# Interleaving attention steps with projection tiles in a two-block transformer kernel on Trainium2: four parts per step instead of two, single-tile slices, and a new home for the head transposes

## What is computed

```python
p = rms_norm(x, g_pre) @ w_in             # q, k, v, gate of three kinds: diff, sb, fox
# per kind, in query blocks of 128 against the keys up to the block's end
# diff: 4 heads of 2 score maps, w = softmax(s0) - lam * softmax(s1); o = w @ v; rms_norm(o)
# sb:   8 heads, a = sigmoid(z) * prod(1 - sigmoid(z)) over later keys; o = a @ v
# fox:  8 heads, softmax(q k + cum_log_f[q] - cum_log_f[k]); o = p @ v
y = concatenate([ya, yb, yc]) @ w_out     # each multiplied by silu(gate) first
x = x + rms_norm(y, g_post)
```

## Time and profile before

| | |
|---|---|
| three runs, median (lowest to highest) | 2060.19 us (2058.29 to 2060.98) |
| the profiled execution: its time, its span | 2059.62 us, 2057.7 us |
| busy: PE, ACT, DVE, POOL | 1945.6, 888.6, 763.3, 660.2 us |
| mean granted clock of PE | 0.963 |

### The profile page before, as it was taken

The page is one execution under the profiler, slowest core; times in us unless marked ns, Lnnn a source line. Parts: engine busy times, 40 slices in busy tenths (PEclk is TensorE's granted clock), DMA queues, the critical chain, the costliest instruction groups (busy, mean ns, idle before and its releaser), DMA issues.

```text
span 2057.7 us, 25679 instructions
## 1 busy us (share of the span) xinstructions
PE 1945.6 (95%) x9552; PEld 1602.4 (78%) x9552; DVE 763.3 (37%) x1393; ACT 888.6 (43%) x1743; POOL 660.2 (32%) x278
## 2 busy tenths in 40 slices
PE   8998998998899899899889989999999999999998
PEld 6876887877777778787777768888778878888886
DVE  3435655344443455534442592101252441111102
ACT  4555454343455555534443562333353353332222
POOL 2422322321233223132024244443302424444442
PEclk9999999997899999999789999999999999999999
DMA  4221111211322122121142222232201332322322
GB/s 148 82 72 52 62 62 52 82 62 59 114 74 72 52 69 65 43 81 62 31 164 82 72 82 93 85 95 92 87 2 52 101 115 92 98 97 94 101 94 91
DMA packets 44572, 163.80 MB, mean 80 GB/s; under 512 B 6192, under 2 KB 6448, under 8 KB 43824
## 3 DMA queue, kind: packets, MB, share of 16 engines
q1 hardware_dynamic: 42640, 148.65, 22.5%
q10 hardware_dynamic: 1824, 13.63, 1.8%
HBM read 155.97 MB, written 6.29 MB: 79 GB/s over the span
## 4 chain that ended last, share of the span: by engine, by line
PE 81%; DVE 10%; ACT 6%; issue 3%; DMA 0%; POOL 0%; DVEq 0%; ACTq 0%; POOLq 0%; SPq 0%
PE bank L586 11%; PE bank L588 11%; PE bank L587 11%; PE bank L589 10%; PE bank L591 10%; PE bank L590 10%; PE bank L699 3%; PE bank L717 2%; PE bank L677 2%; PE bank L723 2%; PE bank L678 1%; ACT q_dup L912 1%; PE bank L719 1%; PE bank L675 1%; PE bank L639 1%
## 5 line engine op out<-in xcount | busy, mean ns | idle before, releaser
L569 POOL TENSOR_TENSOR w_hl<-w_raw,w_hl 128x1024 fp32r<-128x1024 f32 x274 | 660.0, 2413 | 1373.2 <-ACT w_hl L800 1372.6
L800 ACT ACTIVATE w_hl<-w_raw 128x1024 fp32r<-128x1024 f32 x274 | 287.3, 1058 | 349.9 <-DMA w_raw<-wstream 349.5
L586 PE MATMUL bank<-act_hl,w_hl 128*128 128x512 f32 x1056 | 429.0, 406 | 3.7 <-DVE act_hl L1143 2.1
L588 PE MATMUL bank<-act_hl,w_hl 128*128 128x512 f32 x1056 | 414.8, 393 | 0.0
L587 PE MATMUL bank<-act_hl,w_hl 128*128 128x512 f32 x1056 | 414.3, 392 | 0.0
L589 PE MATMUL bank<-w_hl,act_hl 128*128 128x512 f32 x672 | 265.4, 395 | 4.3 <-POOL w_hl L569 2.1
L590 PE MATMUL bank<-w_hl,act_hl 128*128 128x512 f32 x672 | 262.9, 391 | 0.0
L591 PE MATMUL bank<-w_hl,act_hl 128*128 128x512 f32 x672 | 262.8, 391 | 0.0
L586 PEld LDWEIGHTS bank<-act_hl,w_hl 128*128 128x128 f32 x1056 | 200.9, 190 | 47.1 <-issue 3.6
L588 PEld LDWEIGHTS bank<-act_hl,w_hl 128*128 128x128 f32 x1056 | 199.9, 189 | 43.4
L587 PEld LDWEIGHTS bank<-act_hl,w_hl 128*128 128x128 f32 x1056 | 200.8, 190 | 40.7 <-issue 2.2
(11 more groups left out here) (216 smaller groups left out, 2906.2 us busy)
## 6 DMA issues: line engine op xcount, KB each, us to landing
w_raw<-wstream SPq DMA_DIRECT2D x274, 512.0 KB, 3.4
x_spill<-x_res ACTq DMA_DIRECT2D x2, 2048.0 KB, 6.9
x_res<-x_spill ACTq DMA_DIRECT2D x2, 2048.0 KB, 8.0
x_res<-x SPq DMA_DIRECT2D x4, 512.0 KB, 4.9
g_post<-post_gains ACTq DMA_DIRECT2D x4, 512.0 KB, 3.7
x_res<-x ACTq DMA_DIRECT2D x1, 2048.0 KB, 7.7
out<-x_res SPq DMA_DIRECT2D x4, 512.0 KB, 2.6
probs<-w_gates ACTq DMA_DIRECT2D x1, 1024.0 KB, 9.7
```

What stands on the lines that cost most here:

```text
L569: nc.gpsimd.tensor_tensor(w_hl[:, slot, 1].rearrange("p c n -> p (c n)"), w_raw[:, slot, :], w_hl[:, slot, 0].rearrange("p c n -> p (c n)" ...
L586: pe.matmul(out_ap, wh, ah, start=start, stop=False)
L588: return pe.matmul(out_ap, wl, ah, start=False, stop=stop)
L800: nc.scalar.activation(w_hl[:, b % RING, 0].rearrange("p c n -> p (c n)"), w_raw[:, b % RING, :], ACT.Copy).then_inc(s_high_done, 1)
```

## The change

A step of attention gets four parts, with a place for each of PE's four pieces: PART_OF gives the parts of the first transpose, scores, second transpose and values, (0, 1, 2, 3) for the three kinds of the first block and (1, 0, 3, 2) for dil. ACT's and DVE's pieces are placed to match. weave() slices blocks into single tiles and spreads them by a weight that grows with the length of the unit's row. The dense groups are handed out anew among the kinds. The head turn of the first block goes through bank 7, which the values use, ahead of the scores of its step, and its DVE part is split in heads_gate() and heads_low(). ACT writes q once; the second copy is made by two DMAs of 64 partitions x 2 KB per head pair, on ACT's queue, and the scores wait for them.

```diff
-HEADS_AT = {"diff": (10, 13, 16, 18), "sb": (11, 13, 16, 18), "fox": (12, 14, 16, 18), "dil": (8, 13, 17, 18)}
+HEADS_AT = {"diff": (7, 11, 15, 18), "sb": (10, 12, 15, 18), "fox": (14, 15, 16, 18), "dil": (8, 13, 17, 18)}
+ATT_PARTS = 4
+PART_OF = {"diff": (0, 1, 2, 3), "sb": (0, 1, 2, 3), "fox": (0, 1, 2, 3), "dil": (1, 0, 3, 2)}
+    def weight(st):
+
+        if st[0] != "att":
+            return 1
+        unit = st[3] - (1, 0, 1, 2)[st[4]]
+        return 2 + row_tile(st[2], unit) if 0 <= unit < 16 else 1
+
...
-            rest = [half for st in dense_steps
-                    for half in ([st[:4] + ((0, 1),), st[:4] + ((2, 3),)] if st[0] == "block" else [st])]
+            rest = [tile for st in dense_steps
+                    for tile in ([st[:4] + ((j,),) for j in st[4]] if st[0] == "block" else [st])]
             n, seen = sum(st[0] == "block" for st in rest), 0
-            for i, other in enumerate(others[at:upto]):
-                while rest and (seen < math.ceil(n * (i + 1) / (upto - at)) or rest[0][0] != "block"):
+            loads = list(itertools.accumulate(weight(other) for other in others[at:upto]))
+            for other, load in zip(others[at:upto], loads):
+                while rest and (seen < math.ceil(n * load / loads[-1]) or rest[0][0] != "block"):
...
-            if ki == 0:
-                parts = [(project("g", l, 0) + project("v", l, 1), done)]
-            else:
-                parts = [(output(l, ki - 1) + project("qk", l, ki, 1), 15), (project("g", l, ki), done)]
-            parts.append((project("qk", l, ki + 1, 0) if more else [], 2 * ATT_STEPS))
-            steps += weave(parts, attention(l, kind))
-            if ki == 1:
-                steps += project("v", l, 2)
+        parts = [(project("g", l, 0) + project("v", l, 1) + project("qk", l, 1, 0) + project("qk", l, 1, 1), end)]
+        steps += weave(parts, attention(l, "diff"))
+        parts = [(output(l, 0), first_of["sb"] // 2), (project("g", l, 1), first_of["sb"]),
+                 (project("qk", l, 2, 0) + project("v", l, 2), end)]
+        steps += weave(parts, attention(l, "sb"))
+        parts = [(output(l, 1) + project("qk", l, 2, 1), 8 * ATT_PARTS - 1), (project("g", l, 2), first_of["fox"])]
+        early, *late = output(l, 2)
+        parts += [([], ATT_PARTS * (HEADS_AT["fox"][1] + 2)), ([early], end)]
+        steps += weave(parts, attention(l, "fox"))
         steps.append(("xback", l))
-        steps += tile_by_tile(output(l, len(KINDS) - 1))
+        steps += tile_by_tile(late)
...
+            if n in HEADS_AT[kind] and part == (3 if kind == "dil" else 1):
+                p = HEADS_AT[kind].index(n)
+                take(("Y", l, kind, p), BT if kind == "dil" else BO)
...
+        pe.wait_ge(s_q_dup[m], 64 * (len(KINDS) * l + KINDS.index(kind) + 1))
...
-                        for rows in heads_:
-                            ins = nc.scalar.activation(q_dup[rows, p, a, :], ps[heads_[a], :], ACT.Copy, scale=HD ** -0.5)
+                        ins = nc.scalar.activation(q_dup[heads_[a], p, a, :], ps[heads_[a], :], ACT.Copy, scale=HD ** -0.5)
...
+                if j % 2 == 1:
+                    act.wait_ge(s_qk_high, MARKS["qk_high", (g["index"], j - 1)])
+                    for a in range(2):
+                        act.dma_start(q_dup[heads_[1 - a], p, a, :].bitcast(f32), q_dup[heads_[a], p, a, :].bitcast(f32))\
+                            .then_inc(s_q_dup[g["m"]], 16)
...
+                    elif part == 1:
                         if n < 16 and kind == "sb":
                             for a in range(2):
                                 stick(l, kind, n, a)
+                        elif n < 16:
+                            maxima(l, kind, n)
                         if n < 16 and kind == "diff":
                             inverses(l, kind, n)
+                        if n in HEADS_AT[kind]:
+                            heads_gate(l, kind, HEADS_AT[kind].index(n))
```

More of the change, by code:

```diff
@@ L18 @@
+import itertools
 import math
@@ L86, in attention @@
     def attention(l, kind):
-        return [("att", l, kind, n, part) for n in range(ATT_STEPS) for part in range(2)]
+        return [("att", l, kind, n, part) for n in range(ATT_STEPS) for part in range(ATT_PARTS)]
     def project(tag, l, ki, m=0):
```

134 lines of the change are left out of this document (75 added, 59 removed).

## The result

The changed kernel takes 2104.78 us (median of 4 runs, 2103.15 to 2106.2) against 2059.26 us before (4 runs, 2058.29 to 2060.98): a ratio of 1.0222, 95% interval 1.0205 to 1.0238. It is 45 us slower. I had forecast 2062 us with a range up to 2083. One run of all kernels was slow, 3770 us, of the one with copies and full filling; its median of 2038.87 us counts it in and would be 2038.39 without, and its ratio leaves it out.

What follows compares the result with a forecast made beforehand. The prediction took PE to bound the kernel, so only its waits, clock and work count. Terms of -0.9 us per layer, twice -1.8, plus 3.3 for the LRU gave 2061.1 against the profiled 2059.62; forecast 2062 us, range 2037 to 2083.

Steps and rivals of the forecast that it cites:

- the four terms ahead of fox's end: Waits of PE per layer: diff -3.2, border of diff and sb +3.7, sb +2.6, fox up to its last dense tile +1.0 us.
- Returns to dense work: Per layer, 69 more returns from short to dense matmuls at 0.11 us, less cheaper values: plus 4.5 us net, between 3.4 and 7.6.
- Border of diff and sb: Waits of PE there go from 2.6 to 6.3 us per layer: 2.1 for bank 0, 4.2 before sb's first transpose.
- Sb, 10.3 us of waits: PE's waits in sb rise from 7.7 to 10.3 us per layer, the largest 3.7 for bank 7 at step 12.
- Diff, minus 3.2: PE's waits in diff fall from 7.9 to 4.7 us per layer, with sixteen dense blocks spread evenly over nineteen steps.
- Waits at fox's end: Per layer: 5.2 us idle at the gate drain, some 5.5 in steps 14 to 16, 2.3 for the last head pair.
- Clock: Lost clock per layer: 9.0 to 6.8 us in diff and sb; at fox's end 15.2 before, 2.8 after.
- a clock still near 0.6: Sign of being right: the clock at the end of fox stays near 0.6, over a shorter stretch.
- The copies by DMA at nothing: Two DMA issues replace two ACT activations in the drain of q and k; bounds nothing and 1.2 us, taken as nothing.
- The LRU, plus 3.3: Once, at the LRU's end: PE's 8.4 us wait for ACT's gate drain grows by 3.3 us to 11.7.
- Bank 7 becomes the chain: Rival, chance 0.20: values behind head turns wait for DVE's gating, 1.3 us at eight more per layer, 21 us; 2083 us.
- Thin dense loses the clock: Rival, chance 0.03: transposes and short products lose the clock in fox's steps 8 to 16, 19 us more per layer; 2100 us.

## Why the prediction was wrong

**The ladder.** The experiments give a path from before to after. The times are medians of different chips, and the interval of each is about 3.5 us to either side:

| kernel | us | step |
|---|---|---|
| before | 2059.3 | |
| copies of q by DMA | 2046.7 | -12.6 |
| new grouping, head steps, single tiles | 2057.2 | +10.5 |
| head turns through bank 7 | 2051.2 | -6.0 |
| four places for dense tiles | 2095.9 | +44.7 |
| new order per engine | 2085.2 | -10.7 |
| weights | 2104.8 | +19.6 |

The rungs hold for this order only; the slices show by how much a rung can change with what stands around it. The rung of +10.5 is +33.4 for the grouping with its head steps and -22.9 for single tiles. The ladder compares kernels with each other. Which term of my sum was off is another question, and the next list goes by the sum: waits grew by 12.6 us per layer where I had 9.2 (the four terms ahead of fox's end, and 13.0 for 7.9 there), transitions by 3.5 for 4.5, and the clock has the rest.

**Point by point,** per layer:

- *Returns to dense work, plus 4.5 (3.4 to 7.6).* Right. 66 more slices begin at full clock; over its first five matmuls a slice takes 0.10 us more than five later ones; transitions grew by 3.5, less than 66 x 0.10. The price read from the trace held. That the difference is the values' weight load, which I had put at 0.08 without a row, no run shows. The lower price that I had worked out from the Trainium skill's page "TensorE: Matmul & The Clock Gate", section "Back-to-back issue gap", did not show.
- *Border of diff and sb, plus 3.7.* Right: 1.6 us for bank 0 (forecast 2.1) and 4.2 for the first transpose (4.2).
- *Sb, 10.3 us of waits.* The wait for bank 7 at step 12 came (3.6 for 3.7). In all sb waits for 14.0 us behind its first transpose. The row that I missed is the copy of the output product's half on DVE, 2.8 us, right ahead of a tile that needs the bank.
- *Diff, minus 3.2.* Failed. Without the border it waits for 8.7 us by the starts, 9.1 before: 3.4 us at the drain of q and k, where I had counted 2.5, and 2.7 behind the drain of the values, where I had counted nothing. I had walked the chains of the units over PE's work and had checked the banks of dense tiles only where a stage ends.
- *Waits at fox's end.* Right in each part: 5.1 for 5.2, 2.2 for 2.3, 4.7 us of small ones by the starts for 5.5.
- *Clock.* This is the step that failed. "The slow clock adds 2.8 by the share of these idle times" and minus 2.2 in diff and sb gave 14.6 us won per layer; 4.2 were lost. That is 19 of the 21 us by which each layer missed.

  The prediction's own measure says the same: 1 minus the clock, times the stretch, was 0.38 x 40 = 15.2 us at the end of fox, was to become 2.8, and is 15.2 again in the row below. In diff and sb, by the stretches of the result, it is 0.03 x 133 + 0.06 x 155 = 13.3 us for the forecast 6.8. The sum charged the old end of fox with all of its lost clock and the new end with a share, though one of its own signs of being right was a clock still near 0.6 there. I had let steps 14 to 16 go at DVE's pace and so made the clock nearly free.

  The row that spoke against it was there: at a clock of 0.62 PE is busy for 32.2 of the 40 us, DVE for 19.4 and ACT for 15.4, and an engine so busy is not one that waits for the others. Filling the gaps showed it: 6.8 us per layer off fox in the changed kernel, and about 5 in the kernel before. That is half and a third of what the measure counts, so the old 15.2 were not all there to be won either.

  For the rest I had priced three long waits at 2.25 us of clock each; that price rests on four waits above 2.5 us, and the earlier trace rows have three (2.6, 2.6, 2.8), which makes it 3.0. In diff and sb alone there were four stretches of half clock, behind waits of 2.8 to 4.2 us, one of them a wait that I had missed.

The last 40 us of fox in the kernel after, to be read against the earlier trace rows:

```profile
496.00:536.00 40.00, 32.03 (x126) 26.71 (x127) 15.10 (x34) 11.47 (x26) 4.74 (x2) 0.62 0.17 66
```

The four stretches in diff and sb, the last of them behind the values' wait of 3.6 us:

```profile
188.00:201.00 13.00, 9.64 (x36) 7.55 (x36) 9.05 (x17) 8.53 (x19) 2.37 (x1) 0.74 0.28 81
```

```profile
237.00:244.00 7.00, 4.93 (x15) 3.81 (x15) 4.41 (x5) 2.88 (x6) 2.19 (x1) 0.52 0.13 50
271.00:275.00 4.00, 3.67 (x9) 2.96 (x10) 2.51 (x6) 0.00 (x0) 0.82 (x1) 0.57 0.02 4
339.00:346.00 7.00, 5.04 (x16) 4.36 (x17) 3.28 (x6) 1.74 (x3) 2.06 (x1) 0.55 0.01 4
```

- *The copies by DMA at nothing.* Wrong by 12.6 us when they stand alone. I gave ACT's 1.2 us per pair as a bound and took nothing, though the drain of q and k ends one of the two waits of 2.6 us in the earlier trace rows, and I had put it ahead of fox's 3.0 us myself. What they win in the changed kernel was not tried.
- *The LRU, plus 3.3.* The place was right, the size too large: the wait went from 8.4 to 10.1 us.

```profile
PE bank L599 <- ACT x_res L901: 10.1, 1, 10.1
```

Of that part's 3.0 us these are 1.7; the wait for the GELUs ahead of it, 2.1 us for 0.9, is another 1.2.

- *The rivals.* "Bank 7 becomes the chain" ended on the right side for the wrong reason: bank 7 alone wins 6 us with two places, and in the changed kernel bank 6 is 10 us worse. "Thin dense loses the clock" gave a nearer time, 2100, at a chance of 0.03; its price, 19 us per layer, was for steps 8 to 16 of fox, where the clock held up to 496 us. (The row of dil holds transposes mixed with short products, about a quarter of its matmuls, and so says nothing on transposes alone.) What I had no rival for is what costs most on the ladder: dense tiles between the operations of one step. I read the four places only as finer cover, and did not ask which engine's queue holds an instruction for each of those operations in order. DVE's outputs ahead of its scaling were in the order of before.

What stays open: why the weights cost 20 us in the new order, most of it in fox, and nothing in the old (2095.9 without them, 2096.46 with) was measured, not explained. Why the grouping costs 33 us with halves and single tiles then win 23 is open too, and so is the share of the clock in diff and sb, which was read from the trace and not tried.

## What to carry to other kernels

When dense work is put between the operations of a pipeline step, look at the queues of the other engines: an operation that now comes later on PE holds whatever stands behind its reader. Check for each tile which drain frees its bank and how far behind the drain it stands, on the engine that drains. And where an engine is busy for most of a stretch at a low clock, count the low clock as time in the chain until a row shows that another engine is busier; filling its gaps with work that nothing reads is a quick test of that. Read the gain in the stretch that was filled, since the total can move elsewhere too, and do not expect all of the lost clock back.

## What the hardware did that I had not expected

- Filling matmuls of 128x256 in PE's gaps, 0.13 us each in a row of eight, took 6.8 us per layer off fox in the changed kernel and about 5 in the one before, at a granted clock of 1.00 where it had been 0.51 and 0.63. In the kernel before, with waits of 1.0 to 1.4 us from 472 to 500 us and one of 2.6 at 504, the clock was at its lower level for 31 of the 34 us from 473 to 507.
- Two DMAs issued by ACT take 1.12 us on ACT's queue, and its activations beside them start at 203.59 and 204.19, one right behind the other; 48 copies of 128 KB between partition halves landed in 2.8 us (median), and no wait of PE is named after one.
- A table load ahead of a drain is in the wait of the dense tile behind it: in the kernel before with single tiles the tile waited 2.7 us, with a load of 1.28 us and the first gate activation in that time.
